# Opening of a fused two-block transformer kernel: the first slot on the input before its norm, two weight low parts on GpSimd

## The chip, the cores and the metric

One core of a Trainium2 chip runs the whole program in one launch. The metric is the device time of the program in microseconds; the time before is the median of three runs.

## The reference

Two transformer blocks over 256 tokens of width 1024 in float32; the first has 16 meta tokens in front, so T1 = 272 columns. What matters here is the very beginning: the RMS norm of the input, and its product with `w_in`.

```python
def _rmsnorm(x, g):
    y = xf * lax.rsqrt(jnp.mean(xf * xf, axis=-1, keepdims=True) + EPS)
    return (y * g.astype(jnp.float32)).astype(x.dtype)

    h = jnp.concatenate([meta, x], axis=1)
    n = _rmsnorm(h, pre_mix_norm[l])
    proj = jnp.einsum('btd,dn->btn', n, w_in[l])
    (gq, gk, gv, gz, gb, ga, aq, ak, av, iq, ik, iw, gate_a, gate_b) = jnp.split(proj, split_at, axis=-1)
```

The rest is a gated delta rule beside sparse attention, a feed-forward layer, a retention layer, differential attention and two convolved feed-forward layers. Each begins with a product over a normed activation.

## The kernel before

**The weight stream.** All weights come as one stream of slots of 1 MB, 128 partitions by 8 tiles (`KT`) by 256 columns (`STREAM`). Slot 0 ("small") holds the 128 columns of `ik` and 24 of the gates; slots 1 to 12 are `qkv`. A slot lands in one of four raw buffers; SP issues slots 0 to 3 at the start and slot s once TensorE is done with slot s - 4 (`slot_done`, L680).

**High and low parts.** A float32 product is made of three matmuls on rounded operands: high by high, high by low, low by high. ScalarE makes the high part of a slot, `whi` (`load_hi`, L494), VectorE the rest, `wlo = raw - whi` (`load_lo`, L501), written over the raw slot. For six slots in the attention stage GpSimd does the latter (`pool_low`, L699): the counter `lo_ready` goes up in slot order, so whoever makes part s must have part s - 1 counted first. The input is split in the same way into `xhi` and `xlo`.

**The opening.** SP issues the input in two halves (L665), 4 KB of gains (L667), raw slots 0 and 1, the rest of the parameters, the first constants, raw slots 2 and 3 and the other constants (L668 to L675). Tokens are the columns of `h`, the features its 8 tiles, so that the norm's sum runs over partitions: ScalarE squares the input by two tiles at a time (L820), VectorE adds these in pairs (L1283), TensorE sums over partitions with a matrix of ones (L2024), ScalarE takes the root (L822), VectorE the reciprocal `rstd` (L1285). VectorE then scales each tile by its gain and `rstd` into `xf` (L1296), ScalarE rounds two tiles at a time into `xhi` (L780), VectorE subtracts into `xlo` (L1291), in a pipeline of four steps (`xf_mix`, `xhi_mix`, `xlo_mix`). TensorE runs slot 0 step by step as these come (L2038, L2039), then its low weight part (L2043). ScalarE copies the two results out of PSUM (L829, L830), which frees PSUM pair 0. From slot 1 on, `pe_layer` runs `feature_slot` (matmuls at L520), 48 matmuls per slot of 272 columns, on the two PSUM pairs in turn. In `qkv` each result goes through four convolution taps, one on ScalarE (L842), three on VectorE (L1392), which then frees the pair; both make the parts of slot s + 3 in between.

**What sets the order.** Each engine's program is written out by hand; engines meet only by counting semaphores. `keep_warm` (L638) issues matmuls of ones on ones into a free PSUM pair while TensorE waits for the norm: ten ahead of the sums and 18 behind them. In VectorE's program the order is: two sums, the reciprocal, the four steps of scaling and subtracting, then the low parts of slots 0 to 3 (L501), then the convolution. GpSimd fills constants at the start (L2655 to L2659) and then waits for the attention stage.

```python
def pool_low(pool, first, end):
    for s in range(first, end):
        pool.wait_ge(lo_ready, s)
        pool.wait_ge(hi_ready, s + 1)
```

In the feed-forward layers of the second block GpSimd makes a product (L733) and a low part (L737) for each pair of tiles, beside VectorE's convolution taps (L2005) and weight parts (L501).

Of the kernel before, what the change touches and what calls it, by code (L numbers as in the profile page):

```python
# [19 lines left out]
F32 = mybir.dt.float32  # L20
F32R = mybir.dt.float32r
ALU = mybir.AluOpType
# [116 lines left out]
def program(nc, stream, params, const1, const2, x_in, x_tok, gains, y_out):  # L139
    ctx = ExitStack()  # L140
    with ctx:
# [4 lines left out]
        def at(name, off, shape, dt=F32):  # L146
            return nc.alloc_sbuf_tensor_at(name, shape, dt, offset=base + off)
# [75 lines left out]
        pT = at("pT", B + 109568, [P, 2, 3, P])  # L223
        xf = at("xf", B + 83968, [P, KT, T1])
        sq = at("sq", B + 92672, [P, KT, T1])

        sqq = at("sqq", HB, [P, 8, T1])
        sqk = at("sqk", B + 101376, [P, 8, T1])
# [328 lines left out]
        def pe_layer(name, hi, lo, body=4, lead=0, ready=None, pace=2, pre=None):  # L557

            def step(s0, it, j):
                u0 = pair_first[name] + j  # L560
                slot_in(s0, it)
                pair_in(u0, it, body // 2)
                feature_slot(s0, u0 % 2, hi, lo, ready=ready if j == 0 else None, pace=pace).then_inc(slot_done, 1)
                if pre and j == 0:
                    pe_spread(pre)
            slots(nc.tensor, name, step, body, lead=lead)
# [94 lines left out]

        @block.sync
        def _(sp):
            for c in range(2):
                sp.dma_start(h[:, 4 * c:4 * c + 4], x_in[:, 4 * c:4 * c + 4]).then_inc(x_loaded[c], 16)  # L665
            gains = PCOL["conv"]
            sp.dma_start(par[:, 0:gains], params[:, 0:gains]).then_inc(gain_in, 16)  # L667
            sp.dma_start(raw[:, 0], stream[0]).then_inc(w_loaded[0], 16)  # L668
            sp.dma_start(raw[:, 1], stream[1]).then_inc(w_loaded[1], 16)
            sp.dma_start(par[:, gains:NPAR], params[:, gains:NPAR]).then_inc(par_in, 16)  # L670
# [35 lines left out]

        def pool_body(pool, own):

            pool.wait_ge(S("rope"), 6)
            pool_low(pool, FIRST["gb"], FIRST["gb"] + 1)  # L710
            pool.wait_ge(S("rope"), 9)
# [101 lines left out]
        def act_body(act, own):  # L813
            act.wait_ge(set_up, 1)
            nc.scalar.activation(gtmp[:, 2, 0, 1:2], eps[:, 0:1], ACT.Sqrt)
            for c in range(4):
                if c % 2 == 0:
                    act.wait_ge(x_loaded[c // 2], 16)
                a = slice(2 * c, 2 * c + 2)
                nc.scalar.activation(sq[:, a], h[:, a], ACT.Square).then_inc(S("sq_mix"), 1)  # L820
            b = full(act, "norm_mix")
            is_free(nc.scalar.activation(rstd[:], b[:, 0:T1], ACT.Sqrt, scale=1.0 / D, bias=eps[:, 0:1]), "norm_mix")  # L822
            load_hi(0, 0)
            act_high_mix(act)
            load_hi(1, 0)
            load_hi(2, 0)

            act.wait_ge(slot_done, 1)
            nc.scalar.copy(ik[:], PS[0][:, 0, 0:T1])  # L829
            nc.scalar.copy(smf[0:24], PS[0][0:24, 1, 0:T1]).then_inc(pair_free[0], 1)  # L830
            load_hi(3, 0)

            act.wait_ge(par_in, 16)
# [443 lines left out]
        def dve_mix(dve, own):  # L1277


            for n in range(2):  # L1280
                dve.wait_ge(S("sq_mix"), 2 * n + 2)
                a, b = slice(4 * n, 4 * n + 2), slice(4 * n + 2, 4 * n + 4)
                nc.vector.tensor_tensor(sq[:, a], sq[:, a], sq[:, b], ALU.add).then_inc(S("sum_mix"), 1)  # L1283
            after(dve, "norm_mix")
            own.link(nc.vector.reciprocal(rstd[:], rstd[:]))  # L1285
            dve.wait_ge(gain_in, 16)

            def low(c):
                dve.wait_ge(S("xhi_mix"), c + 1)
# [11 lines left out]
            for c in range(4):  # L1301
                if c < 3:
                    scaled(c + 1)
                low(c)

        def dve_layer_out(dve, own, name, pre=None):

# [68 lines left out]

        def dve_body(dve, own):
            dve_mix(dve, own)
            load_lo(0, 0)
            load_lo(1, 0)  # L1380
            load_lo(2, 0)
            load_lo(3, 0)
            dve.wait_ge(par_in, 16)
# [633 lines left out]
        def pe_norm_mix(pe):  # L2017

            b = fill("norm_mix")
            keep_warm("small", 10)  # L2020
            for kt in (0, 1, 4, 5):
                if kt % 4 == 0:
                    pe.wait_ge(S("sum_mix"), kt // 4 + 1)
                ins = nc.tensor.matmul(b[:, 0:T1], ones[:], sq[:, kt], start=kt == 0, stop=kt == 5)  # L2024
            is_full(ins, "norm_mix")
            keep_warm("small", 18)

        def pe_small(pe):


            u = slice(0, P), slice(P, P + 24)
            out = PS[0][:, 0, 0:T1], PS[0][0:24, 1, 0:T1]
            pe.wait_ge(hi_ready, 1)
            for c in range(4):
                pe.wait_ge(S("xlo_mix"), c + 1)
                for t in range(2):
                    for kt in (2 * c, 2 * c + 1):
                        nc.tensor.matmul(out[t], whi[:, 0, kt, u[t]], xhi[:, kt], start=kt == 0, stop=False)  # L2038
                        nc.tensor.matmul(out[t], whi[:, 0, kt, u[t]], xlo[:, kt], start=False, stop=False)  # L2039
            slot_in(0, 0)  # L2040
            for t in range(2):
                for kt in range(KT):
                    ins = nc.tensor.matmul(out[t], wlo[:, 0, kt, u[t]], xhi[:, kt], start=False, stop=kt == KT - 1)  # L2043
            ins.then_inc(slot_done, 1)

        def pe_body(pe):
            pe.wait_ge(set_up, 1)
# [763 lines left out]
```

## Time and profile before

| | |
|---|---|
| median of 3 runs | 1336.21 us (1334.67 to 1336.22) |
| profiled execution, its own time | 1335.83 us |
| its span | 1334.0 us |
| granted TensorE clock, mean | 0.997 |
| busy: TensorE, VectorE, ScalarE, GpSimd | 98%, 68%, 52%, 9% |

The span runs from the first instruction to the last; the time of the program is 1.8 us longer. Times in the rows are microseconds from the span's start. PE is TensorE, DVE VectorE, ACT ScalarE, POOL GpSimd, SP the engine that issues most DMAs (its queue is SPq). A row of the timeline gives the start, the length of the group, engine, line, operation, output and inputs, how many instructions the group has, and in brackets the idle time ahead of it and what ended that.

### The profile page before, as it was taken

How to read it: one execution, taken by the hardware profiler on the slowest of the kernel's cores; microseconds unless marked ns; L12 is line 12 of the kernel's file. 1: busy time of each engine (PE TensorE's matmuls, PEld its weight loads, DVE VectorE, ACT ScalarE, POOL GpSimd, SP SyncE). 2: the span in 40 equal slices, each digit the busy share in tenths (PEclk: the TensorE clock that was granted, in tenths of full speed). 3: DMA queues.
4: the chain of work that ended last, by engine and by line, in shares of the span. 5: the costliest groups of instructions: out<-in, count | busy, mean ns of one | idle time of the engine just before them, and what ended most of it. 6: DMA issues, size and time to landing. Idle time of an engine off the chain costs nothing.

```text
span 1334.0 us, 24352 instructions
## 1 busy us (share of the span) xinstructions
PE 1310.1 (98%) x9497; PEld 1217.3 (91%) x9497; DVE 907.2 (68%) x1192; ACT 689.9 (52%) x1017; POOL 119.0 (9%) x111
## 2 busy tenths in 40 slices
PE   8999999999999999999999999999999999999997
PEld 7997999999998999888999887999987998999986
DVE  6886763667656877446854456778756786899954
ACT  5655355533234544335344564666645567766652
POOL 0000151000000000000000000222300000134410
PEclk9999999999999999999999999999999999999999
DMA  7452332410055555554554345455565444455562
GB/s 288 166 182 95 127 127 96 136 54 13 20 190 197 176 179 179 188 189 161 185 205 158 127 161 186 161 186 189 189 208 180 165 143 158 159 182 178 179 232 95
DMA packets 30313, 213.01 MB, mean 160 GB/s; under 512 B 3488, under 2 KB 3616, under 8 KB 5152
## 3 DMA queue, kind: packets, MB, share of 16 engines
q1 hardware_dynamic: 29088, 206.72, 44.7%
q0 software_dynamic: 1152, 5.24, 1.2%
q8 instruction: 55, 0.90, 0.3%
q14 instruction: 18, 0.15, 0.0%
HBM read 210.90 MB, written 1.05 MB: 159 GB/s over the span
## 4 chain that ended last, share of the span: by engine, by line
PE 88%; DVE 7%; ACT 3%; issue 1%; DMA 1%; DVEq 0%; SPq 0%; ACTq 0%
PE lin L520 54%; PE lin L599 20%; PE aux L2308 2%; PE aux L2322 2%; PE aux L2320 1%; DVE wlo L501 1%; PE lin L2597 1%; PE aux L2198 1%; ACT lm L1167 1%; DVE ht L1332 1%; ACT whi L494 1%; PE aux L2454 1%; PE aux L2270 1%; DVE iscore L1441 1%; ACT xhi L755 0%
## 5 line engine op out<-in xcount | busy, mean ns | idle before, releaser
L501 DVE TENSOR_TENSOR wlo<-raw,whi 128x2048 fp32r<-128x2048 f32 x187 | 434.7, 2328 | 200.4 <-ACT whi L494 200.0
L520 PE MATMUL lin<-xhi,whi 128*128 128x256 f32 (+1 forms) x1648 | 470.8, 286 | 1.4 <-DVE xlo L1343 1.4
L494 ACT CAST whi<-raw 128x2048 fp32r<-128x2048 f32 x193 | 367.1, 1905 | 198.1 <-DMA raw<-in_stream 168.7
L520 PE MATMUL lin<-xlo,whi 128*128 128x256 f32 (+1 forms) x1648 | 466.0, 283 | 0.0
L520 PE MATMUL lin<-xhi,wlo 128*128 128x256 f32 (+1 forms) x1648 | 463.7, 281 | 0.0
L520 PEld LDWEIGHTS lin<-xhi,whi 128*128 128x128 f32 x1648 | 310.0, 188 | 4.2 <-issue 2.6
L520 PEld LDWEIGHTS lin<-xhi,wlo 128*128 128x128 f32 x1648 | 311.9, 189 | 0.0
L520 PEld LDWEIGHTS lin<-xlo,whi 128*128 128x128 f32 x1648 | 310.5, 188 | 0.4
L520 PE MATMUL lin<-whi,xhi 128*128 128x256 f32 (+1 forms) x344 | 99.5, 289 | 0.6 <-DVE xlo L1343 0.4
L520 PE MATMUL lin<-wlo,xhi 128*128 128x256 f32 (+1 forms) x344 | 96.6, 281 | 0.0
L520 PE MATMUL lin<-whi,xlo 128*128 128x256 f32 (+1 forms) x344 | 96.4, 280 | 0.0
L2005 DVE SCALAR_TENSOR_TENSOR ft<-fy,par,ft 128x254 f32<-128x254 f32 (+1 forms) x176 | 91.0, 557 | 5.9 <-DVE ft L2005 0.2
L733 POOL TENSOR_TENSOR fu<-fs,ft 128x256 f32<-128x256 f32 x44 | 48.7, 1107 | 249.1 <-ACT fs L1269 249.1
L599 PE MATMUL lin<-whi,flo 128*128 128x512 f32 x176 | 70.2, 399 | 0.0
L599 PE MATMUL lin<-wlo,fhi 128*128 128x512 f32 x176 | 69.4, 394 | 0.0
L599 PE MATMUL lin<-whi,fhi 128*128 128x512 f32 x176 | 69.0, 392 | 0.0
L1261 ACT ACTIVATE ft<-fy,par 128x256 f32<-128x256 f32 x88 | 48.2, 594 | 38.4 <-DVE fy L1997 36.7
L520 PEld LDWEIGHTS lin<-whi,xhi 128*128 128x128 f32 (+1 forms) x344 | 64.1, 186 | 2.3 <-issue 1.5
L520 PEld LDWEIGHTS lin<-wlo,xhi 128*128 128x128 f32 (+1 forms) x344 | 64.0, 186 | 1.2 <-issue 1.0
L520 PEld LDWEIGHTS lin<-whi,xlo 128*128 128x128 f32 (+1 forms) x344 | 63.9, 186 | 0.2
L599 PE MATMUL lin<-whi,ulo 128*128 128x512 f32 x128 | 51.1, 399 | 0.0
L737 POOL TENSOR_TENSOR flo<-fu,fhi 128x256 f32 (+1 forms) x44 | 38.7, 879 | 137.5 <-ACT fhi L1248 137.5
(419 smaller groups left out, 2023.4 us busy)
## 6 DMA issues: line engine op xcount, KB each, us to landing
raw<-in_stream SPq DMA_DIRECT2D x193, 1024.0 KB, 4.9
gp<-in_gains POOLq DMA_DIRECT2D x6, 512.0 KB, 3.9
c<-in_const SPq DMA_DIRECT2D x1, 1652.0 KB, 17.9
h<-in_x SPq DMA_DIRECT2D x2, 544.0 KB, 4.2
c<-in_const POOLq DMA_DIRECT2D x1, 1024.0 KB, 5.2
ht<-in_xtok POOLq DMA_DIRECT2D x1, 1024.0 KB, 10.8
out<-ht SPq DMA_DIRECT2D x1, 512.0 KB, 2.6
out<-ht SPq DMA_DIRECT2D x2, 256.0 KB, 2.2
```

The lines of the kernel that those rows point to most:

```text
L494: nc.scalar.copy(whi[:, s0 % 4], raw[:, s0 % 4]).then_inc(hi_ready, 1)
L501: nc.vector.tensor_tensor(wlo[:, s0 % 4], raw[:, s0 % 4], whi[:, s0 % 4].bitcast(F32), ALU.subtract).then_inc(lo_ready, 1)
L520: ins = nc.tensor.matmul(out, a, b, start=start and n == 0, stop=stop and n == 2)
L599: ins = nc.tensor.matmul(PS[u % 2][:, c], a, b[:, kt - 4 * g], start=kt == 0 and n == 0, stop=kt == kts - 1 and n == 2)
L733: nc.gpsimd.tensor_tensor(fu[:, s0 % 2], fs[:, s0 % 2], ft[:, s0 % 2, 1], ALU.mult)\
L737: nc.gpsimd.tensor_tensor(flo[:, bass.ds(j + 4 * it, 1)], fu[:, s0 % 2].unsqueeze(1), fhi[:, bass.ds(j + 4 * it, 1)].bitcast(F32), ALU.sub ...
L1167: ins = nc.scalar.activation(lm2s[t][:, q, 0:W], lm2s[t][:, q, 0:W], ACT.Exp, bias=dmax[:, t, q:q + 1], accum_out=dsum[:, t, q:q + 1])
L1261: ins = nc.scalar.activation(ft[:, p, t], fy[:, p, t], ACT.Identity, scale=pdyn(f"f_conv{k}", (t * FT2 + j) * 3 + 2 + 12 * it), bias=pdyn( ...
L1332: nc.vector.scalar_tensor_tensor(ht[:, c, f], yt[:, c, f], rc[:, c:c + 1], ht[:, c, f], ALU.mult, ALU.add).then_inc(S("h_" + tag), 1)
L2005: ins = nc.vector.scalar_tensor_tensor(ft[:, p, t, sh:SEQ], fy[:, p, t, 0:SEQ - sh], pdyn(f"f_conv{k}", col), ft[:, p, t, sh:SEQ], ALU.mul ...
L2308: ins = nc.tensor.matmul(b[:, q * P:q * P + P], als[a][:, p_], tus[a][:, p_ // 2, p_ % 2], start=True, stop=True)
L2322: ins = nc.tensor.matmul(b[:, (2 + q) * P:(3 + q) * P], xss[a][:, p_], tus[a][:, g, 2 + q], start=True, stop=True)
```

## The change

The gains are loaded ahead of the input. ScalarE no longer squares all the input: it writes `ghi0`, the high part of input times gain, without the norm, and squares one of four pairs of tiles; VectorE squares the other three and makes the low part `glo0`. TensorE runs slot 0 on `ghi0` and `glo0`, tile by tile, and VectorE multiplies the two results by `rstd` as it copies them out of PSUM, in place of ScalarE. The low parts of slots 0 and 1 are made by GpSimd. ScalarE makes the high parts of slots 1 and 2 ahead of `xhi`. Slot 1 goes tile by tile behind `xlo_mix`, all high-weight matmuls first and the low-weight ones last. VectorE waits for `lo_ready` 2 before it makes the low part of slot 2. All 18 keep-warm matmuls stand ahead of the sums.

```diff
@@ -223,6 +223,8 @@
         pT = at("pT", B + 109568, [P, 2, 3, P])
         xf = at("xf", B + 83968, [P, KT, T1])
         sq = at("sq", B + 92672, [P, KT, T1])
+        ghi0 = at("ghi0", B + 43520, [P, KT, T1], F32R)
+        glo0 = at("glo0", B + 52224, [P, KT, T1], F32R)
 
         sqq = at("sqq", HB, [P, 8, T1])
         sqk = at("sqk", B + 101376, [P, 8, T1])
@@ -558,6 +560,9 @@
 
             def step(s0, it, j):
                 u0 = pair_first[name] + j
+                if s0 == FIRST["qkv"] and j == 0:
+                    pe_first_feature(nc.tensor, s0, u0 % 2).then_inc(slot_done, 1)
+                    return
                 slot_in(s0, it)
                 pair_in(u0, it, body // 2)
                 feature_slot(s0, u0 % 2, hi, lo, ready=ready if j == 0 else None, pace=pace).then_inc(slot_done, 1)
@@ -661,10 +666,10 @@
 
         @block.sync
         def _(sp):
+            gains = PCOL["conv"]
+            sp.dma_start(par[:, 0:gains], params[:, 0:gains]).then_inc(gain_in, 16)
             for c in range(2):
                 sp.dma_start(h[:, 4 * c:4 * c + 4], x_in[:, 4 * c:4 * c + 4]).then_inc(x_loaded[c], 16)
-            gains = PCOL["conv"]
-            sp.dma_start(par[:, 0:gains], params[:, 0:gains]).then_inc(gain_in, 16)
             sp.dma_start(raw[:, 0], stream[0]).then_inc(w_loaded[0], 16)
             sp.dma_start(raw[:, 1], stream[1]).then_inc(w_loaded[1], 16)
             sp.dma_start(par[:, gains:NPAR], params[:, gains:NPAR]).then_inc(par_in, 16)
@@ -706,6 +711,7 @@
 
         def pool_body(pool, own):
 
+            pool_low(pool, 0, 2)
             pool.wait_ge(S("rope"), 6)
             pool_low(pool, FIRST["gb"], FIRST["gb"] + 1)
             pool.wait_ge(S("rope"), 9)
@@ -813,21 +819,21 @@
         def act_body(act, own):
             act.wait_ge(set_up, 1)
             nc.scalar.activation(gtmp[:, 2, 0, 1:2], eps[:, 0:1], ACT.Sqrt)
+            act.wait_ge(gain_in, 16)
             for c in range(4):
                 if c % 2 == 0:
                     act.wait_ge(x_loaded[c // 2], 16)
-                a = slice(2 * c, 2 * c + 2)
-                nc.scalar.activation(sq[:, a], h[:, a], ACT.Square).then_inc(S("sq_mix"), 1)
+                for kt in (2 * c, 2 * c + 1):
+                    ins = nc.scalar.activation(ghi0[:, kt], h[:, kt], ACT.Copy, scale=pcol("pre_mix", kt))
+                ins.then_inc(S("ghi0"), 1)
+                if c == 1:
+                    nc.scalar.activation(sq[:, 0:2], h[:, 0:2], ACT.Square).then_inc(S("sq_mix"), 1)
+            load_hi(0, 0)
             b = full(act, "norm_mix")
             is_free(nc.scalar.activation(rstd[:], b[:, 0:T1], ACT.Sqrt, scale=1.0 / D, bias=eps[:, 0:1]), "norm_mix")
-            load_hi(0, 0)
-            act_high_mix(act)
             load_hi(1, 0)
             load_hi(2, 0)
-
-            act.wait_ge(slot_done, 1)
-            nc.scalar.copy(ik[:], PS[0][:, 0, 0:T1])
-            nc.scalar.copy(smf[0:24], PS[0][0:24, 1, 0:T1]).then_inc(pair_free[0], 1)
+            act_high_mix(act)
             load_hi(3, 0)
 
             act.wait_ge(par_in, 16)
@@ -1277,13 +1283,33 @@
         def dve_mix(dve, own):
 
 
+            def squares(c):
+                a = slice(2 * c, 2 * c + 2)
+                return nc.vector.tensor_tensor(sq[:, a], h[:, a], h[:, a], ALU.mult)
+
+            def raw_low(c):
+                dve.wait_ge(S("ghi0"), c + 1)
+                for kt in (2 * c, 2 * c + 1):
+                    ins = nc.vector.scalar_tensor_tensor(glo0[:, kt], h[:, kt], pcol("pre_mix", kt),
+                                                         ghi0[:, kt].bitcast(F32), ALU.mult, ALU.subtract)
+                ins.then_inc(S("glo0"), 1)
+
+            dve.wait_ge(x_loaded[0], 16)
+            squares(1)
+            dve.wait_ge(gain_in, 16)
+            raw_low(0)
+            raw_low(1)
+            dve.wait_ge(x_loaded[1], 16)
+            squares(2)
+            own.link(squares(3))
+            dve.wait_ge(S("sq_mix"), 1)
             for n in range(2):
-                dve.wait_ge(S("sq_mix"), 2 * n + 2)
-                a, b = slice(4 * n, 4 * n + 2), slice(4 * n + 2, 4 * n + 4)
+                a, b = slice(2 * n, 2 * n + 2), slice(2 * n + 4, 2 * n + 6)
                 nc.vector.tensor_tensor(sq[:, a], sq[:, a], sq[:, b], ALU.add).then_inc(S("sum_mix"), 1)
+            raw_low(2)
+            raw_low(3)
             after(dve, "norm_mix")
             own.link(nc.vector.reciprocal(rstd[:], rstd[:]))
-            dve.wait_ge(gain_in, 16)
 
             def low(c):
                 dve.wait_ge(S("xhi_mix"), c + 1)
@@ -1302,6 +1328,10 @@
                 if c < 3:
                     scaled(c + 1)
                 low(c)
+            dve.wait_ge(slot_done, 1)
+            nc.vector.tensor_tensor(ik[:], PS[0][:, 0, 0:T1], rstd[:], ALU.mult)
+            nc.vector.tensor_tensor(smf[0:24], PS[0][0:24, 1, 0:T1], rstd[0:24], ALU.mult).then_inc(pair_free[0], 1)
+            dve.wait_ge(lo_ready, 2)
 
         def dve_layer_out(dve, own, name, pre=None):
 
@@ -1376,8 +1406,6 @@
 
         def dve_body(dve, own):
             dve_mix(dve, own)
-            load_lo(0, 0)
-            load_lo(1, 0)
             load_lo(2, 0)
             load_lo(3, 0)
             dve.wait_ge(par_in, 16)
@@ -2017,13 +2045,12 @@
         def pe_norm_mix(pe):
 
             b = fill("norm_mix")
-            keep_warm("small", 10)
-            for kt in (0, 1, 4, 5):
-                if kt % 4 == 0:
-                    pe.wait_ge(S("sum_mix"), kt // 4 + 1)
-                ins = nc.tensor.matmul(b[:, 0:T1], ones[:], sq[:, kt], start=kt == 0, stop=kt == 5)
+            keep_warm("small", 18)
+            for kt in range(4):
+                if kt % 2 == 0:
+                    pe.wait_ge(S("sum_mix"), kt // 2 + 1)
+                ins = nc.tensor.matmul(b[:, 0:T1], ones[:], sq[:, kt], start=kt == 0, stop=kt == 3)
             is_full(ins, "norm_mix")
-            keep_warm("small", 18)
 
         def pe_small(pe):
 
@@ -2031,17 +2058,34 @@
             u = slice(0, P), slice(P, P + 24)
             out = PS[0][:, 0, 0:T1], PS[0][0:24, 1, 0:T1]
             pe.wait_ge(hi_ready, 1)
-            for c in range(4):
-                pe.wait_ge(S("xlo_mix"), c + 1)
-                for t in range(2):
-                    for kt in (2 * c, 2 * c + 1):
-                        nc.tensor.matmul(out[t], whi[:, 0, kt, u[t]], xhi[:, kt], start=kt == 0, stop=False)
-                        nc.tensor.matmul(out[t], whi[:, 0, kt, u[t]], xlo[:, kt], start=False, stop=False)
+            for part, name in ((ghi0, "ghi0"), (glo0, "glo0")):
+                for kt in range(KT):
+                    if kt % 2 == 0:
+                        pe.wait_ge(S(name), kt // 2 + 1)
+                    for t in range(2):
+                        nc.tensor.matmul(out[t], whi[:, 0, kt, u[t]], part[:, kt], start=name == "ghi0" and kt == 0, stop=False)
             slot_in(0, 0)
             for t in range(2):
                 for kt in range(KT):
-                    ins = nc.tensor.matmul(out[t], wlo[:, 0, kt, u[t]], xhi[:, kt], start=False, stop=kt == KT - 1)
+                    ins = nc.tensor.matmul(out[t], wlo[:, 0, kt, u[t]], ghi0[:, kt], start=False, stop=kt == KT - 1)
             ins.then_inc(slot_done, 1)
+
+        def pe_first_feature(pe, s, pair):
+
+            pe.wait_ge(hi_ready, s + 1)
+            for kt in range(KT):
+                if kt % 2 == 0:
+                    pe.wait_ge(S("xlo_mix"), kt // 2 + 1)
+                for t in range(2):
+                    for x in (xhi, xlo):
+                        nc.tensor.matmul(PS[pair][:, t, 0:T1], whi[:, s % 4, kt, t * P:t * P + P], x[:, kt],
+                                         start=kt == 0 and x is xhi, stop=False)
+            slot_in(s, 0)
+            for t in range(2):
+                for kt in range(KT):
+                    ins = nc.tensor.matmul(PS[pair][:, t, 0:T1], wlo[:, s % 4, kt, t * P:t * P + P], xhi[:, kt],
+                                           start=False, stop=kt == KT - 1)
+            return ins
 
         def pe_body(pe):
             pe.wait_ge(set_up, 1)
```

## Rows read from the trace of the kernel before

**Rows 1.** The page, busy time: engine, us, share of the span, instructions.
```profile
PE 1310.1 (98%) x9497; PEld 1217.3 (91%) x9497; DVE 907.2 (68%) x1192; ACT 689.9 (52%) x1017; POOL 119.0 (9%) x111
```

**Rows 2.** Chain of waits, first 60 us: start, us, what.
```profile
9.66 1.86 DVE rstd L1285
11.55 1.74 DVE xf L1296 x4
...
17.65 2.21 DVE wlo L501
...
19.91 2.27 PE lin L2043 x16
22.17 37.92 PE lin L520 x301
```

**Rows 3.** What TensorE waits for, whole span: us in total, times, longest.
```profile
PE aux L616 <- DVE ht L1332: 4.0, 7, 1.3
```

**Rows 4.** SP's issues (start, us), and single issues with us to landing.
```profile
1.68 0.42 SPq L667 DMA_DIRECT2D par<-in_params  x1
2.14 0.43 SPq L668 DMA_DIRECT2D raw<-in_stream  x1
...
4.11 0.99 SPq L674 DMA_DIRECT2D raw<-in_stream  x2
...
raw<-in_stream SPq DMA_DIRECT2D x1, 1024.0 KB, 7.5
...
raw<-in_stream SPq DMA_DIRECT2D x1, 1024.0 KB, 11.7
```

**Rows 5.** ScalarE, the opening in order of time: start, us, count.
```profile
4.54 1.20 ACT L820 ACTIVATE sq<-h 128x544 f32<-128x544 f32 x2 [2.29 <-DMA h<-in_x]
...
9.14 0.49 ACT L822 ACTIVATE rstd<-aux,eps 128x272 f32<-128x272 f32 x1 [2.03 <-PE aux L2024]
9.68 1.90 ACT L494 CAST whi<-raw 128x2048 fp32r<-128x2048 f32 x1
12.50 0.65 ACT L780 CAST xhi<-xf 128x544 fp32r<-128x544 f32 x1 [0.92 <-DVE xf L1296]
```

**Rows 6.** VectorE, the same: the first low part of the input.
```profile
13.20 0.72 DVE L1291 TENSOR_TENSOR xlo<-xf,xhi 128x544 fp32r<-128x544 f32 x1
```

**Rows 7.** TensorE, the same: keep-warm and norm matmuls (two records each).
```profile
1.21 4.35 PE L638 MATMUL lin<-ones 128*128 128x128 f32 x20 [1.21 <-POOL small L2659]
6.55 1.18 PE L2024 MATMUL aux<-sq,ones 128*128 128x272 f32 x4 [0.99 <-DVE sq L1283]
...
8.94 4.18 PE L638 MATMUL lin<-ones 128*128 128x128 f32 x36
```

**Rows 8.** GpSimd's weight parts, min/median/max; a VectorE operation beside the first.
```profile
L699 POOL TENSOR_TENSOR wlo<-raw,whi x6: 4545/4568/4607, 156.4 to 206.0; 128x2048 fp32r<-128x2048 f32 x6
...
157.32 0.45 DVE L1440 MAX8 top<-iscore 128x8 f32<-128x272 f32 x1
```

**Rows 9.** GpSimd, then VectorE, late feed-forward stage: start, us, count.
```profile
1191.74 0.74 POOL L733 TENSOR_TENSOR fu<-fs,ft 128x256 f32<-128x256 f32 x1 [1.20 <-ACT fs L1269]
...
1197.53 2.87 POOL L733 TENSOR_TENSOR fu<-fs,ft 128x256 f32<-128x256 f32 x1 [1.28 <-ACT fs L1269]
...
1191.81 2.83 DVE L501 TENSOR_TENSOR wlo<-raw,whi 128x2048 fp32r<-128x2048 f32 x1
...
1197.51 2.28 DVE L501 TENSOR_TENSOR wlo<-raw,whi 128x2048 fp32r<-128x2048 f32 x1
1199.71 2.91 DVE L2005 SCALAR_TENSOR_TENSOR ft<-fy,par,ft 128x255 f32<-128x255 f32 x4
```

**Rows 10.** Stretches: busy us (records) by engine, granted clock, DMA share, GB/s.
```profile
139.00:141.00 2.00, 2.00 (x10) 1.88 (x9) 1.13 (x2) 1.09 (x1) 0.00 (x0) 0.50 0.00 0
142.00:144.00 2.00, 2.00 (x19) 2.00 (x19) 1.90 (x5) 0.00 (x0) 0.00 (x0) 1.00 0.00 0
...
1330.00:1333.00 3.00, 0.00 (x0) 0.00 (x0) 1.42 (x4) 0.00 (x0) 0.00 (x0) 0.50 0.80 316
```

## The prediction

> **What bounds the kernel now.** I read the page first: TensorE is busy 98% of the span, no other engine is above 68% [rows 1]. Then the chain of waits of the first 60 us: from 22.17 us on it is TensorE alone, without a gap [rows 2]; before that it runs over the input's DMA, the norm, the reciprocal, the scaling on VectorE and the low part of the first weight slot. The list of what TensorE waits for says the same of the rest: the longest single wait of the whole span is 1.3 us [rows 3]. So the opening is a prologue to 1,300 us of matmuls, and what the first slots gain or lose in time is carried to the end nearly one to one. All that follows asks one thing: when does TensorE begin slot 2 of the stream, from which on it again has work without a pause? Now: slot 1 begins at 22.17 and has 48 matmuls at 37.92 / 301 = 0.126 us each [rows 2], so slot 2 begins at 28.2.
>
> **The change part by part.**
>
> *DMA order.* SP issues the 4 KB of gains first, 0.46 us ahead of the two halves of the input (the issue is 0.42 us, the next comes 0.46 later) [rows 4]. The first half, now there at 4.54 [rows 5], comes at 5.0. Raw slot 0 is issued where it was and lands at 2.14 + 7.5 = 9.64 [rows 4]; behind the same bytes, with at most those 0.46 us lost ahead of them, it lands between 9.64 and 10.1: I take 9.9. Raw slot 2, 4.11 + 11.7 = 15.8, comes at 16.1.
>
> *ScalarE.* It drops four squares over 544 columns (0.6 us each) and keeps one, and adds eight scaled copies over 272 columns; between the 0.3 that the columns' share of a square would be and the 0.49 of the root of the same width I take 0.35, 2.8 us in all [rows 5]. From 5.0 that is over at 8.4, before raw slot 0 is there, so it costs nothing. The high part of slot 0 then takes 9.9 to 11.8 (1.90) [rows 5].
>
> *VectorE, first half.* Three squares, two sums (0.72 each) and eight low parts over 272 columns (0.42 each as for the scaling, 1.74 for four) [rows 2, 6]: both sums are done at about 10.3, the last low part at 12.05. TensorE's norm matmuls (1.18 a pair) [rows 7] end near 11.7; the root follows the high part of slot 0, 11.8 to 12.3; the reciprocal (1.86) [rows 2] ends at 14.2. Now it ends at 11.52.
>
> *TensorE, slot 0.* The norm is out of its way: 32 matmuls on the raw input's two parts, 4.0 us, from 11.8 to 15.8 (the keep-warm matmuls, 4.35 us for ten and twice as fast later [rows 7], end near 7.3 and stand before the norm). Then it needs the low weight part, which GpSimd now makes: 4.57 us [rows 8] against VectorE's 2.21 [rows 2].
>
> *GpSimd beside VectorE: the term that decides.* In the feed-forward stage both make two-input operations out of SBUF, and the rows show them excluding each other. GpSimd alone takes 0.74 for its product; issued 0.02 us behind VectorE's weight subtraction of 2.28 it took 2.87, that is until 0.6 after the other's end; and the VectorE subtraction issued 0.07 behind GpSimd's 0.74 took 2.83 in place of 2.28. Behind the first of these the next VectorE operations, already queued at 1199.71, let GpSimd through first [rows 9]. So one blocks the other for a whole operation, in order of arrival. The six weight parts that GpSimd makes in the kernel before do not show it: they all run at 4.55 to 4.61 [rows 8]. The Trainium skill, page "SBUF — State Buffer", section "Who interferes with whom", states this as an exclusive lock of a shared port pair, held for the whole instruction, which a VectorE instruction with two SBUF inputs needs against a GpSimd one that reads SBUF; the trace agrees (2.87 for 0.74), and by this rule the change is worth less than a count of operations says.
>
> Placed in time: GpSimd is ready for slot 0 at 11.8, gets in behind the last low part at 12.05 and ends at 16.5. VectorE's scaling (input and reciprocal, both in SBUF) is ready at 14.2, waits until 16.5, and its first instruction ends at 16.8. GpSimd has meanwhile asked for slot 1 (its high part is done near 14.3) and goes next: 16.8 to 21.2. The second scaling instruction ends at 21.5. From there all is as now, where ScalarE starts its first high part at 12.50 when that instruction has ended [rows 5] and VectorE is done with the fourth low part at 17.65 [rows 2]: 5.15 us, so the fourth low part is there at 26.65. ScalarE's high part of slot 2 (16.1 to 18.0), which the change moves ahead of the input's high parts, is over by then.
>
> *TensorE, slots 0 to 2.* Slot 0's low part at 16.5, its 16 matmuls (2.27) [rows 2] done at 18.8, now 22.17. Slot 1's first 32 matmuls go by twos of the input's tiles; the last 8 start at 26.65 and take 1.0, its 16 low ones 2.0: 29.7. VectorE behind the fourth low part makes the two moved copies (0.9 by the scaling's rate) and the low part of slot 2 (2.3): 29.9. Slot 2 starts at 29.9 in place of 28.2: **+1.7**. Next late would be the convolution of slot 1 on VectorE, which must free the pair before slot 3: about 35.2 against 35.9, so it holds, by 0.7 us. SP asks for slot 4 at 18.8, 3.4 us earlier than now; nobody waits for it.
>
> *The clock.* TensorE stands from 18.8 to about 23.0 (21.5 plus the 1.44 from the second scaling to the first low part, 12.48 to 13.92), 4.2 us, longer than any wait of now. At the end of the span, with TensorE idle, the granted clock reads 0.50; and where it was 0.50 in 139 to 141, TensorE got 10 matmuls into two microseconds in place of 19, until it read 1.00 again by 142 [rows 10]. So slot 1 probably starts at 1.2 GHz. One such stretch costs nothing where TensorE waits for the input's parts anyway (3.0 us of work in 23.0 to 26.65) and up to 1.6 if all of it falls on work: I take +0.6.
>
> *What no row shows:* the reciprocal (one SBUF input) beside a GpSimd operation. If it is free of it, 0; if it too waits until 16.5, GpSimd's second operation comes behind it at 18.2 and all is 1.8 later. I take 0, since single-input VectorE work, such as the maximum at 157.32, ran at 0.45 beside a GpSimd part and left its time alone [rows 8].
> By the same section of the Trainium skill's page "SBUF — State Buffer" an instruction with one SBUF input outside the two-port modes does not contend; no run here shows it for a reciprocal.
>
> **Sum:** 1.7 + 0.6 = +2.3 on the profiled execution's 1335.83 (span 1334.0 and 1.8 around it): 1338.1; that execution lies 0.4 under the median of 1336.21, so 1338.5 as a median. About 0.2%, 2.7 us, is what a measurement here can tell from no change, so this is just inside.
>
> **Rivals.**
> *The clock decides* (slower). Same chain, but TensorE stays at 1.2 GHz well into slot 1. At twice 0.126 us it does 22 matmuls in 5.6 us from 23.0, the other 26 take 3.3: 31.9, which is +3.7 in place of +1.7, and with the spread 1340.3. It passes 0.2% when the low clock lasts over about 4.5 us after 23.0. For it: 4.2 us of standing still. Against: in the middle of the kernel it was back by 142 [rows 10], a few microseconds on.
> *The reciprocal waits too:* +1.8 on the forecast, 1340.3.
> *No blocking* (not slower). If GpSimd's long operations leave VectorE alone, the input's parts are ready behind the high part of slot 2: 18.0 plus 5.15 is 23.15; slot 1 ends at 26.2, slot 2 starts behind VectorE's copies and its low part at 26.4: −1.8, so 1334.4. For it: all six GpSimd times are equal. Against: VectorE then ran work with one SBUF input, as the maximum at 157.32 [rows 8], and where both had two, they blocked each other [rows 9].
> *VectorE keeps the port for all four first scalings:* GpSimd then comes in at 18.2 while VectorE waits for ScalarE, ends at 22.6, and the fourth low part is at 26.9: the forecast again, within 0.3.
>
> **How the numbers follow.** Forecast, with the last rival in it, 0.5, spread 1336.5 to 1340; the clock 0.2; the reciprocal 0.08; no blocking 0.12; the rest 0.1, something unseen in the first 30 us that leaves it within 0.2%. Slower by over 0.2% (above 1338.9): a third of the forecast's cases and the two rivals, 0.17 + 0.2 + 0.08 = 0.45. Faster by over 0.2% (below 1333.5) needs no blocking and 0.9 more than it gives: 0.03. Within: 0.52. Range 1335.2 to 1341.2: it leaves out most of "no blocking" and the far end of the clock's case.
>
> **What would show it.** Right: GpSimd's two operations from about 12 to 21.2, the second near 4.7 long with one scaling instruction of about 2.6 and one of about 4.8 beside them on VectorE; the fourth low part of the input at 26 to 27; a TensorE gap of about 4 us after slot 0 and a granted clock of 0.50 behind it; slot 2 at 29.9 to 30.5; from there on every stage as now. Wrong: scaling instructions of 0.5 us while GpSimd runs, low parts of the input at 19 to 23, and slot 2 at 26.4; or a difference that arises after 60 us.

## The result and the profile after

The changed kernel takes 1340.01 us (median of 14 runs, 1336.85 to 1340.51) against 1336.09 us of the kernel before on the same chips (14 runs, 1334.24 to 1336.37): 3.9 us slower, a ratio of 1.0027 with a 95% interval of 1.0018 to 1.0035. Its profiled execution took 1338.48 us, one of the lower ones, with a span of 1336.7.

First the page's busy times, as [rows 1]. Nothing has changed in the whole: TensorE is still the bound.

```profile
PE 1308.9 (98%) x9477; PEld 1216.5 (91%) x9477; DVE 917.0 (69%) x1203; ACT 690.9 (52%) x1020; POOL 128.4 (10%) x113
```

The chain of waits of the first 60 us, as [rows 2]: start, us, what.

```profile
10.65 10.25 DVE glo L1293 x4
...
20.90 1.77 DVE rstd L1312
...
22.70 1.74 DVE xf L1322 x4
...
28.05 2.27 PE lin L2081 x16
30.32 2.00 PE lin L2086 x16
32.32 27.68 PE lin L522 x221
```

The reader is to see the first line: four VectorE instructions of 0.42 us each hold the chain for 10.25 us. The reciprocal, at 9.66 before, starts at 20.9. The last line is where TensorE begins slot 2 and no longer pauses: 32.3, where [rows 2] give 22.17 + 48 x 0.126 = 28.2. The opening is 4.1 us longer, and the medians differ by 3.9: the loss arises in the first 33 us.

What the engines did there, in order of time: SP's raw slot 0 with its time to landing, as [rows 4]; then ScalarE as [rows 5], GpSimd, VectorE and TensorE as [rows 7].

```profile
raw<-in_stream SPq DMA_DIRECT2D x1, 1024.0 KB, 7.1
```

```profile
7.40 1.75 ACT L827 ACTIVATE ghi<-h,par 128x272 fp32r<-128x272 f32 x4
9.23 1.90 ACT L496 CAST whi<-raw 128x2048 fp32r<-128x2048 f32 x1
```

```profile
11.28 9.32 POOL L704 TENSOR_TENSOR wlo<-raw,whi 128x2048 fp32r<-128x2048 f32 x2 [10.14 <-ACT whi L496]
```

```profile
10.57 10.34 DVE L1293 SCALAR_TENSOR_TENSOR glo<-h,par,ghi 128x272 fp32r<-128x272 f32 x4
20.82 1.84 DVE L1312 RECIPROCAL rstd<-rstd 128x272 f32<-128x272 f32 x1
...
27.27 1.53 DVE L1317 TENSOR_TENSOR xlo<-xf,xhi 128x544 fp32r<-128x544 f32 x2
...
29.42 4.47 DVE L503 TENSOR_TENSOR wlo<-raw,whi 128x2048 fp32r<-128x2048 f32 x2
```

```profile
14.01 1.66 PE L2066 MATMUL lin<-glo,whi 128*128 128x272 f32 x12
20.96 1.27 PE L2066 MATMUL lin<-glo,whi 128*128 128x272 f32 x4 [5.29 <-DVE glo L1293]
22.03 3.19 PE L2070 MATMUL lin<-ghi,wlo 128*128 128x272 f32 x16
```

Raw slot 0 landed at 2.14 + 7.1 = 9.24, ScalarE was done with the raw input's high parts by then and made that of slot 0 at once, 9.23 to 11.13. GpSimd started at 11.28, while VectorE was in the second of its last four low parts of the raw input. The third waited for the whole of GpSimd's first operation, the fourth for the whole of its second (two operations, 9.32 us; four low parts, 10.34 in place of 1.74), and the reciprocal, which is next in VectorE's program, waited for both. The view of that line, from 9 us on, has the single ones, min/median/max in ns:

```profile
L1293 DVE SCALAR_TENSOR_TENSOR glo<-h,par,ghi x4: 498/2617/4852, 10.6 to 16.2; 128x272 fp32r<-128x272 f32 x4
```

The shortest is a plain 0.5 us, the longest 4.35 more, nearly a GpSimd operation. TensorE stood for 5.3 us within slot 0 for the last pair of low parts, the longest wait of the span, where [rows 3] had 1.3:

```profile
PE lin L2066 <- DVE glo L1293: 5.3, 1, 5.3
```

The granted clock fell behind that pause, and the 16 low-weight matmuls of slot 0 took 3.19 us in place of 2.27. Two stretches of the changed kernel, as [rows 10]:

```profile
21.00:24.00 3.00, 3.00 (x13) 2.79 (x14) 2.96 (x5) 0.35 (x1) 0.00 (x0) 0.50 0.00 0
138.00:146.00 8.00, 6.88 (x49) 5.84 (x48) 6.14 (x18) 3.78 (x6) 0.00 (x0) 1.00 0.37 132
```

The profile before showed 0.50 in 139 to 141. The same work comes 4.1 us later here, in 143 to 145, and it is at full clock, as all of the second row is. That hides 1.4 us of the loss in this execution: 2.65 us between the two profiled executions, 4.1 at slot 2.

### The profile page after: what moved, and what is told of

It is laid out like the page before. It is cut to its first block, busy times and chain, and to the rows that moved or that the text cites. A ratio compares the mean times of both kernels' runs of the same rounds, so it can differ in the third digit from the quotient of the medians.

```text
span 1336.7 us, 24334 instructions
## 1 busy us (share of the span) xinstructions
PE 1308.9 (98%) x9477; PEld 1216.5 (91%) x9477; DVE 917.0 (69%) x1203; ACT 690.9 (52%) x1020; POOL 128.4 (10%) x113
## 4 chain that ended last, share of the span: by engine, by line
PE 86%; DVE 8%; ACT 3%; DMA 1%; issue 1%; DVEq 0%; SPq 0%; ACTq 0%
PE lin L522 53%; PE lin L604 19%; PE aux L2352 2%; PE aux L2366 2%; PE aux L2364 1%; DVE wlo L503 1%; PE lin L2641 1%; PE aux L2242 1%; DVE glo L1293 1%; DMA raw<-in_stream 1%; ACT whi L496 1%; DVE ht L1362 1%; ACT lm L1173 1%; PE aux L2498 1%; PE aux L2314 1%
## 5 line engine op out<-in xcount | busy, mean ns | idle before, releaser
L503 DVE TENSOR_TENSOR wlo<-raw,whi 128x2048 fp32r<-128x2048 f32 x185 | 430.1, 2328 | 199.7 <-ACT whi L496 199.1
L522 PE MATMUL lin<-xhi,whi 128*128 128x256 f32 (+1 forms) x1632 | 465.3, 285 | 1.4 <-DVE xlo L1373 1.4
L522 PE MATMUL lin<-xlo,whi 128*128 128x256 f32 (+1 forms) x1632 | 460.9, 282 | 0.0
L522 PE MATMUL lin<-xhi,wlo 128*128 128x256 f32 (+1 forms) x1632 | 458.7, 281 | 0.0
L522 PEld LDWEIGHTS lin<-xhi,whi 128*128 128x128 f32 x1632 | 306.4, 188 | 3.9 <-issue 2.6
L522 PEld LDWEIGHTS lin<-xhi,wlo 128*128 128x128 f32 x1632 | 308.4, 189 | 0.0
L522 PEld LDWEIGHTS lin<-xlo,whi 128*128 128x128 f32 x1632 | 306.9, 188 | 0.3
L704 POOL TENSOR_TENSOR wlo<-raw,whi 128x2048 fp32r<-128x2048 f32 x8 | 36.7, 4584 | 175.1 <-DVE aq L1441 149.1
```

The costliest lines, as they stand in the source:

```text
L503: nc.vector.tensor_tensor(wlo[:, s0 % 4], raw[:, s0 % 4], whi[:, s0 % 4].bitcast(F32), ALU.subtract).then_inc(lo_ready, 1)
L522: ins = nc.tensor.matmul(out, a, b, start=start and n == 0, stop=stop and n == 2)
L704: nc.gpsimd.tensor_tensor(wlo[:, s % 4], raw[:, s % 4], whi[:, s % 4].bitcast(F32), ALU.subtract)\
```

## The experiments

Every kernel ran beside the kernel before on the same chip (its medians there: 1335.9 to 1336.1 us). Besides the time I read the start of slot 2 from the chain (before 28.2, changed 32.3), since single runs of most kernels here fall on steps some 1.6 us apart. What those steps are is told under e9.

**e1: GpSimd starts behind the raw input's low parts.**

```diff
+            pool.wait_ge(S("glo0"), 4)
             pool_low(pool, 0, 2)
```

> The changed kernel, but GpSimd waits for all low parts of the raw input before its first weight part, so it can't come in between them. Theory (GpSimd's two operations block every VectorE operation with two SBUF inputs, and in the changed kernel the reciprocal fell in behind both): GpSimd starts at about 12.1, the reciprocal runs at 12.7 to 14.5 beside it, only the scaling waits; slot 2 starts at 29.9 to 30.2 in place of 32.2, about 1337.8 as a median. Rival A (a reciprocal can't run beside a GpSimd operation either): it ends at 18.4, slot 2 at about 32, 1339.8. Rival B (the new order of the opening costs, not GpSimd): 1340 as the changed kernel.

Measured: 1339.79 us (10 runs), ratio 1.0028 (1.0018 to 1.0038). GpSimd, VectorE and two stretches of the granted clock:

```profile
12.17 9.30 POOL L704 TENSOR_TENSOR wlo<-raw,whi 128x2048 fp32r<-128x2048 f32 x2 [11.02 <-DVE glo L1294]
```

```profile
13.31 1.85 DVE L1313 RECIPROCAL rstd<-rstd 128x272 f32<-128x272 f32 x1 [1.23 <-ACT rstd L834]
15.20 7.40 DVE L1323 SCALAR_TENSOR_TENSOR xf<-h,par,rstd 128x272 f32<-128x272 f32 x4
```

```profile
20.00:23.00 3.00, 0.00 (x0) 0.00 (x0) 3.00 (x4) 1.01 (x2) 1.47 (x1) 1.00 0.91 285
24.70:28.00 3.30, 3.25 (x14) 3.25 (x15) 3.23 (x7) 2.49 (x3) 0.00 (x0) 0.50 0.00 0
```

The reciprocal ran beside GpSimd in 1.85 us, as alone: rival A is out, and what the Trainium skill's page "SBUF — State Buffer" says of instructions with one SBUF input ("Who interferes with whom") is now shown for it. The scaling waited as the forecast had it: four instructions took 7.40 us together in place of 1.74. The input's fourth low part was there at 26.96 (forecast 26.65, changed kernel 28.80). But the 1.8 us won on VectorE did not arrive: TensorE idled from 20 to 23 and slot 1 then ran half of its way at 1.2 GHz. Slot 2 started at 31.5, only 0.8 earlier. My 1337.8 missed by 2. (This execution also had the clock at 0.50 from 11.0 to about 14.8, and the reciprocal 0.8 us later than e9 has it below. It cost nothing: the fourth low part is at 26.96 here and at 26.98 in e9, since GpSimd's block outlasts it.)

**e2: no GpSimd in the opening.** VectorE makes both low parts, the rest of the change stays.

```diff
-            pool_low(pool, 0, 2)
...
             raw_low(3)
+            load_lo(0, 0)
...
+            load_lo(1, 0)
             dve.wait_ge(slot_done, 1)
```

> The changed kernel without GpSimd in the opening: VectorE makes the low part of slot 0 behind the low parts of the raw input, that of slot 1 behind the normed input's. Theory: nothing blocks VectorE, the fourth low part of the normed input is there at 22.5 in place of 28.8, slot 2 starts at 27.8 (before: 28.2), 1335.7. Rival B (the new order itself costs): slot 2 at 30 or later, 1338 or more. Rival C (the clock): a low stretch remains and the time stays above 1337.

Measured: 1334.26 us (10 runs), ratio 0.9992 (0.9982 to 1.0002). The weight part in its new place and the start of slot 2:

```profile
11.99 2.29 DVE L503 TENSOR_TENSOR wlo<-raw,whi 128x2048 fp32r<-128x2048 f32 x1
14.20 1.85 DVE L1312 RECIPROCAL rstd<-rstd 128x272 f32<-128x272 f32 x1
```

```profile
27.32 32.71 PE lin L522 x259
```

Slot 2 starts at 27.3 (27.8 expected), 0.9 ahead of the kernel before and 5.0 ahead of the changed one; the time is 1.4 us under the expected 1335.7. So the new order of the opening and the raw input cost nothing; rival B is out, and rival C too. All of the loss is in those two GpSimd operations.

**e3: the clock kept up in the pause.** 21 matmuls of ones into the other PSUM pair, ahead of the last pair of low parts.

```diff
                 for kt in range(KT):
+                    if name == "glo0" and kt == 6:
+                        keep_warm("small", 21, slot=1)
```

> The changed kernel with 21 keep-warm matmuls into the other PSUM pair in TensorE's gap between the sixth and the seventh low part of slot 0. Theory: slot 0's low-weight matmuls take 2.3 us in place of 3.2, but slot 1 waits for the input's low parts all the same; slot 2 starts at 32.2 as in the changed kernel, median 1340. Rival C (the clock is a part of the loss): slot 2 at 31.2 or earlier, 1339 or less.

Measured: 1338.42 us (10 runs), ratio 1.0020 (1.0011 to 1.0030). The low-weight matmuls of slot 0, and the start of slot 2:

```profile
21.48 2.15 PE L2072 MATMUL lin<-ghi,wlo 128*128 128x272 f32 x16
```

```profile
32.23 27.81 PE lin L522 x222
```

In the profile both halves of the expectation hold: 2.15 us in place of 3.19, and slot 2 at 32.2 all the same, because slot 1 waits for VectorE. The median does not, and by its time alone rival C would have won: it is 1.6 us under the changed kernel's, with runs at 1336.5 (3), 1338.4 (3), 1340.0 (3) and 1341.2. The traced execution is one of those at 1340.0, with a stretch at half clock from 142 to 145; 1338.4 would be the same without that stretch (see e9). Why three runs were at 1336.5 is open.

**e4: GpSimd's work without its purpose.** The kernel of e2, and GpSimd squares the input into a dead tile twice, released by the same events.

```diff
+            for c in range(2):
+                pool.wait_ge(x_loaded[c], 16)
+            for s in range(2):
+                pool.wait_ge(hi_ready, s + 1)
+                own.link(nc.gpsimd.tensor_tensor(idle[:], h[:, :, 0:NCOL], h[:, :, 0:NCOL], ALU.mult))
```

ScalarE also waits for these two ahead of the convolution, when they are long done.

> The kernel of e2_vector_lows, where GpSimd makes nothing that is needed, plus two GpSimd products of 128 by 2048 of the input with itself into a dead tile, released by the same two events as its weight parts in the changed kernel. Theory (the port is the cause, not who makes the low part): the last two low parts of the raw input take near 5 us each, everything on VectorE is some 8 us later, slot 2 at about 36, 1344. Rival D (late low weight parts are the cause, GpSimd beside VectorE is harmless): as e2, 1335.7.

Measured: 1342.40 us (4 runs), ratio 1.0045 (1.0028 to 1.0062).

```profile
11.21 7.35 POOL L719 TENSOR_TENSOR idle<-h 128x2048 f32<-128x2048 f32 x2 [10.06 <-ACT whi L497]
...
10.42 8.45 DVE L1299 SCALAR_TENSOR_TENSOR glo<-h,par,ghi 128x272 fp32r<-128x272 f32 x4
```

```profile
34.10 25.94 PE lin L523 x205
```

Nobody needs the result, and still the four low parts take 8.45 us and slot 2 starts at 34.1, 6.8 us behind e2. Rival D is out: it is the running beside each other that costs. The amount was less than expected because a product of the input with itself takes GpSimd 3.6 to 3.7 us, not 4.6.

**e5: the kernel before, with GpSimd's part of the change alone.**

```diff
+            pool_low(pool, 0, 2)
             pool.wait_ge(S("rope"), 6)
...
-            load_lo(0, 0)
-            load_lo(1, 0)
+            dve.wait_ge(lo_ready, 2)
             load_lo(2, 0)
```

> The kernel before with one part of the change alone: GpSimd makes the low parts of slots 0 and 1, VectorE waits for both before that of slot 2. Theory: GpSimd comes in behind the first scaling instruction at about 12, the second ends at 16.5, the input's fourth low part at 21.7, the high part of slot 1 at 22.9, its low part at 27.4, slot 2 starts at 33.5: plus 5.3 us, 1341.4. Rival D (GpSimd beside VectorE is harmless): the input's parts as before, the low part of slot 1 at 23.2, slot 2 at 29.3: plus 1.1, 1337.2.

Measured: 1340.33 us (5 runs, three at 1340.1 to 1340.3 and two at 1344.6 and 1345.2, the latter the profiled one), ratio 1.0039 (1.0025 to 1.0053).

```profile
11.65 4.50 POOL L699 TENSOR_TENSOR wlo<-raw,whi 128x2048 fp32r<-128x2048 f32 x1 [10.50 <-ACT whi L494]
23.24 4.58 POOL L699 TENSOR_TENSOR wlo<-raw,whi 128x2048 fp32r<-128x2048 f32 x1 [7.09 <-ACT whi L494]
...
11.60 6.08 DVE L1297 SCALAR_TENSOR_TENSOR xf<-h,par,rstd 128x272 f32<-128x272 f32 x4
```

```profile
28.50:31.50 3.00, 3.00 (x16) 3.00 (x15) 3.00 (x2) 1.58 (x3) 0.00 (x0) 0.50 0.63 268
```

The places came out within 0.5 us of the expectation: scaling 6.08 us in place of 1.74, the low part of slot 1 ready at 27.8. The extra in the slower two goes with the clock: their mean granted clock is 0.993, that of the other three 0.996 or 0.997. The profile has it at 0.50 while slot 1 runs, so that slot 2 starts near 35.5 (33.5 expected), and once more from about 145 to 151, twice as long as in the kernel before. One detail is new: the first scaling instruction started 0.05 us ahead of GpSimd and was blocked all the same; the timeline cut down to it:

```profile
11.60 4.84 DVE L1297 SCALAR_TENSOR_TENSOR xf<-h,par,rstd 128x272 f32<-128x272 f32 x1
```

The median is 1.1 us under the expectation.

**e6: the same work in 16 pieces.**

```diff
-            pool_low(pool, 0, 2)
+            for s in range(2):
+                pool.wait_ge(hi_ready, s + 1)
+                for kt in range(KT):
+                    ins = nc.gpsimd.tensor_tensor(wlo[:, s, kt], raw[:, s, kt], whi[:, s, kt].bitcast(F32), ALU.subtract)
+                ins.then_inc(lo_ready, 1)
```

> The changed kernel with each of GpSimd's two weight parts cut into 8 operations of 128 by 256. Theory (one whole operation blocks, in order of arrival): no VectorE instruction waits longer than about 0.6 us; the reciprocal starts near 13, but scaling and subtracting take turns with GpSimd; slot 2 at 29.5 to 31, 1337.5 to 1339. Rival (the blocking is by the amount that GpSimd reads, however it is cut): the reciprocal ends at 22 as before, slot 2 at 32 or later, 1340 or more.

Measured: 1337.50 us (10 runs), ratio 1.0014 (1.0005 to 1.0023).

```profile
11.09 14.62 POOL L717 TENSOR_TENSOR wlo<-raw,whi 128x256 fp32r<-128x256 f32 x16 [9.94 <-ACT whi L496]
...
10.37 2.69 DVE L1297 SCALAR_TENSOR_TENSOR glo<-h,par,ghi 128x272 fp32r<-128x272 f32 x4
12.99 1.84 DVE L1316 RECIPROCAL rstd<-rstd 128x272 f32<-128x272 f32 x1
14.86 3.17 DVE L1326 SCALAR_TENSOR_TENSOR xf<-h,par,rstd 128x272 f32<-128x272 f32 x4
```

```profile
29.62 30.44 PE lin L522 x243
```

GpSimd now needs 14.6 us instead of 9.3, VectorE's four low parts 2.69 and four scalings 3.17 instead of 10.34 in one place, and slot 2 starts 2.7 us earlier than in the changed kernel, still 1.4 behind the kernel before. The engines take turns, operation by operation: the slowest of the four low parts took 0.98 us in place of 0.50. What a VectorE instruction waits is one GpSimd operation, however long that is.

**e7: GpSimd for slot 0 only**, released as in e1; VectorE makes the low part of slot 1.

```diff
-            pool_low(pool, 0, 2)
+            pool.wait_ge(S("glo0"), 4)
+            pool_low(pool, 0, 1)
...
+            dve.wait_ge(lo_ready, 1)
+            load_lo(1, 0)
             dve.wait_ge(slot_done, 1)
```

> The changed kernel with GpSimd making the low part of slot 0 only, released when the raw input's low parts are done; VectorE makes that of slot 1 behind the normed input's. Theory: one operation blocks, from 12.1 to 16.7; the second scaling instruction ends at 17.3, the fourth low part at 22.5, slot 2 starts at 27.9, 1335.8: no better than VectorE alone, since the reciprocal hides most of it. Rival B (the new order costs): 1338 or more.

Measured: 1334.83 us (10 runs), ratio 0.9995 (0.9985 to 1.0004), slot 2 at 27.9 as expected:

```profile
27.89 32.20 PE lin L522 x255
```

With one operation, most of it beside VectorE's wait for the norm and the reciprocal, the loss is gone. It gives nothing over e2, where VectorE does all itself (27.3).

**e8: another use of TensorE's pauses.** The kernel before, VectorE's program untouched; ScalarE makes the high part of slot 1 in four pieces between the input's high parts, TensorE feeds slots 0 and 1 together.

```diff
                 nc.scalar.copy(xhi[:, a], xf[:, a]).then_inc(S("xhi_mix"), 1)
+                nc.scalar.copy(whi[:, 1, a], raw[:, 1, a]).then_inc(hi_ready if c == 3 else S("hi_one"), 1)
...
+                for t in range(2):
+                    for kt in (2 * c, 2 * c + 1):
+                        for x in (xhi, xlo):
+                            nc.tensor.matmul(PS[1][:, t, 0:T1], whi[:, 1, kt, t * P:t * P + P], x[:, kt],
+                                             start=kt == 0 and x is xhi, stop=False)
```

The 16 low-weight matmuls of slot 1 follow those of slot 0, and ScalarE copies slot 0's results behind the high part of slot 3.

> The kernel before, with slots 0 and 1 fed together: ScalarE makes the high part of slot 1 in four pieces between the input's high parts, and TensorE runs slot 1's high-weight matmuls behind slot 0's at each step of the input, then both low weight parts; VectorE's program is unchanged. Theory (what bounds the opening is VectorE's chain up to 17.65, and the gaps of TensorE behind it can be filled): slot 2 starts at 26.1 to 26.5 in place of 28.2, 1334.3. Rival (the pieces delay the input's high parts or the first slots run into the low weight parts): 28 or later, 1336.

Measured: 1334.15 us (11 runs, 1332.37 to 1336.92), ratio 0.9989 (0.9980 to 0.9998). The chain:

```profile
22.26 1.99 PE lin L2061 x16
24.25 2.00 PE lin L2066 x16
26.24 33.82 PE lin L520 x270
```

Slot 2 starts at 26.2, 2.0 us ahead of the kernel before, as expected, with TensorE working from 14.0 on without a pause. Five runs are at 1332.4 to 1332.5, 1.6 us under the lowest of the kernel before. It beats both kernels, the kernel before by little.

**e9: e1 with the clock kept up between slots 0 and 1.**

```diff
             ins.then_inc(slot_done, 1)
+            keep_warm("small", 16, slot=1)
```

> The kernel of e1_gpsimd_later with 16 keep-warm matmuls into the other PSUM pair between slot 0 and slot 1. In e1 slot 1 ran half at 1.2 GHz (25 of 48 matmuls' time at a granted clock of 0.50) and the first convolution tap of slot 1 came at 31.7. Theory (the forecast's chain was right once GpSimd starts late, and the clock took 1 us more): slot 1's matmuls all at 0.125 us each, that tap at 30.4 to 30.7, the median about 1 us below e1's 1339.8: 1338.0 to 1338.8. Rival (the clock's stretch is absorbed in waits for the input's parts): the tap at 31.7, 1339.8.

Measured: 1336.89 us (11 runs), ratio 1.0018 (1.0009 to 1.0027).

```profile
30.50 29.56 PE lin L522 x236
```

Slot 2 starts at 30.5, 1.0 us ahead of e1, and slot 1's first tap at 30.65: the theory. The median fell by 2.9, more than the 1.0 to 1.8 expected. The runs show why: six lie at 1336.6 to 1336.9, three at 1338.3 to 1338.8, two at 1339.7 and 1339.9. The traced ones tell what a step is. Near 140 us the clock may be at full speed (changed kernel, above), low for a while (e9), or low for twice as long (e4):

```profile
138.00:146.00 8.00, 6.90 (x37) 5.93 (x37) 6.25 (x14) 2.88 (x5) 0.00 (x0) 0.79 0.30 119
```

```profile
140.00:150.00 10.00, 8.90 (x40) 7.21 (x40) 7.92 (x22) 3.77 (x6) 0.00 (x0) 0.66 0.30 106
```

From the start of slot 2 the span goes on for 1305.8 us before, 1306.1 in e1 (span 1337.6) and 1306.0 in e3 and e9 (span 1336.5), which all have one such stretch, and for 1304.4 us in the changed kernel and 1304.5 in e6 and e8 (1330.7), which have none: about 1.5 us. e7, with the stretch, and e2, without it, lie half a microsecond higher and 1.6 apart (1306.6, 1305.0). e4, with the long one, has 1308.0.

That the untraced runs differ in the same way is not seen in a profile, but their mean granted clocks agree: in the changed kernel 0.993 to 0.995 in the eight runs near 1340.2 and 0.996 or 0.997 in the six below 1339; in e7 0.997 in the four near 1336.3 and 0.998 or 0.999 in the six near 1334.7. So how often a kernel meets that stretch moves its median by up to a step. It covers that e9's median fell by more than the 1.0 us at slot 2, and that e2's gained 1.8 us where its slot 2 gained 0.9: most of its runs are on the lower step, 0.4 us under the lower step of the kernel before (1334.2, 1334.6). The loss of the changed kernel is about the same on either step: 1338.5 against 1334.6, and 1340.2 against 1336.1. One of its 14 runs, at 1336.85, fits neither and stays open.

## Why the prediction was right, and where it was not

The measured 1340.01 lies in the range of 1335.2 to 1341.2 and on the forecast's side of 1336.2. Its size was short: +2.3 forecast, +3.9 measured, past the 0.2% within which I had called it likeliest. By the number alone two rivals, the clock and the reciprocal, both at 1340.3, came nearer than the forecast. Neither is what happened (e1, e3): that the range held rests in part on its width.

*The opening is carried to the end one to one:* right, to within the stretch near 140 us. Slot 2 moved by 4.1 us and the medians by 3.9; e8 shows the same for a gain (2.0 and 1.8), while e3 and e9, with 4.0 and 2.3 at slot 2, lost 2.3 and 1.0 in the median.

*GpSimd and VectorE exclude each other, for a whole operation:* right, and now shown in this place. e4 has the cost with a result that nobody needs, e2 has it gone, e6 shows that the unit is the single operation. The FFN stage of the kernel before [rows 9] was enough to see it, and the rival "no blocking" is refuted.

*"GpSimd is ready for slot 0 at 11.8, gets in behind the last low part at 12.05":* this step failed. I took raw slot 0 to land at 9.9, from a bound that let the gains' DMA only delay it; it landed at 9.24, ahead of its 9.64 before. GpSimd was ready at 11.28, 1.0 us before the last low part would have been done (10.57 + 1.74), and came in with two of the four still to go. The forecast stood on a margin of a quarter of a microsecond, 11.8 against 12.05; the lower end of my own bracket for the landing, 9.64, gives 11.54. Two things followed: those two took the blocking in place of the first two scalings, and the reciprocal, which I had rightly taken to run beside GpSimd (1.85 us in e1), was queued behind them. That is its 1.85 us on the path: the input's fourth low part was there at 28.80 in place of 26.65. With GpSimd's start moved to where the step had it, e1 gives 26.96, so 0.3 of the difference is not this step's. Nor does this step alone make the miss in the time: e1 has GpSimd start where the forecast had it and took 1339.8, in large part because of the clock (below). I had not asked what VectorE had left to do in program order if GpSimd came half a microsecond sooner.

*The last term of the path, slot 1 and the low part of slot 2 behind the fourth low part:* forecast 3.25 us to slot 2, measured 3.5. I had VectorE's copies and low part as its end; they were over at about 31.6, and TensorE itself set it. It began the third pair's eight matmuls at 28.05 and had not finished them when the fourth low part came.

*The clock, +0.6:* the mechanism is right, its place and size are not. The pause came within slot 0 (5.3 us) instead of behind it, the low stretch fell on slot 0's low-weight matmuls, 0.9 us, and these have room: e3 shows slot 2 unmoved without it. In the changed kernel this term is 0. In the schedule that I had forecast it is real: e1 against e9 is 1.0 us at slot 2 (31.5, 30.5). And the stretch near 140 us that the profile before had and this one had not was in no term at all; it is about as large as the whole error of the sum.

*ScalarE's, SP's and the moved copies' work hidden:* right. The moved copies took 0.70 us, 28.72 to 29.42, of the 0.9 that I had them at.

## What to carry to other kernels

Before VectorE's work goes to an idle GpSimd, look for what VectorE does beside it: where both read two operands out of SBUF they take turns by whole operations, and a long GpSimd operation costs most beside short, dependent VectorE ones. If it has to be, release GpSimd where VectorE waits or has one-input work (e7), or cut its work into pieces (e6); here the first gained nothing over VectorE doing it all, and the second still lost 1.5 us. On an in-order engine half a microsecond in the release moves the block onto whatever is queued next, so work the sum out for both sides of each neighbour.

## What was not expected of the hardware

A VectorE instruction that starts first does not always go first: in e5 the scaling started 0.05 us ahead of GpSimd's operation and took 4.84 us, while in [rows 9] the subtraction that started 0.02 us ahead won. The Trainium skill's page "SBUF — State Buffer" gives the port to whoever issues first ("Who interferes with whom"); by the starts in the profile that holds in [rows 9] and not in e5, and a margin of 0.05 us in a profile is not enough to tell who will be first.

A short transfer issued first (4 KB of gains, landed 1.8 us after its issue) did not delay the ones behind it: raw slot 0, issued at 2.14 in all of them, took 7.1 us to land in the changed kernel and 6.7 to 7.2 in the seven other kernels with the new order (7.2 in e7), against 7.5 in the kernel before, 7.4 in e5 and 7.2 in e8, which have the old order. With one profile each, and 7.2 on both sides, this is no proof that the order helps.
